# A token norm's factors one tile behind the evictions, low weights ahead of both, and sums a quarter into the second panel

## The reference, cut to what matters

```python
x = x + rms_norm(jnp.einsum("bse,ed->bsd", mix, w_out[layer]), attn_post_g[layer])
h2 = rms_norm(x, ffn_pre_g[layer])
f = conv_ffn(h2, w_up[layer], conv_w[layer], conv_b[layer], w_down[layer])
x = x + rms_norm(f, ffn_post_g[layer])
# the second block begins with rms_norm_2(x, g) and its input projection
```

## Time and profile before

| | us |
|---|---|
| median of 3 runs | 1391.78 (1391.68 to 1392.61) |
| the profiled execution | 1388.91 |
| its span, first to last instruction | 1386.8 |
| TensorE busy | 1317.0, 95% of the span |
| VectorE busy | 854.3, 62% |
| ScalarE busy | 579.3, 42% |
| GpSimd busy | 218.5, 16% |
| mean granted TensorE clock | 0.981 of full speed |

### The profile page before, as it was taken

How to read it: one execution, slowest core, us unless ns; L and a number is a source line. 1 busy time by engine, 2 the same in 40 slices (tenths; PEclk the granted TensorE clock), 3 DMA queues, 4 the chain that set the end, 5 groups by cost and what they waited for, 6 DMA issues and landing times.

```text
span 1386.8 us, 16092 instructions
## 1 busy us (share of the span) xinstructions
PE 1317.0 (95%) x5982; PEld 1031.8 (74%) x5982; DVE 854.3 (62%) x1497; ACT 579.3 (42%) x872; POOL 218.5 (16%) x173
## 2 busy tenths in 40 slices
PE   7999988899999999999999999899799989999996
PEld 6776656788888888888888868687678855658885
DVE  6355753788887388648853612569987256663342
ACT  5345645544333243224422534323564246653321
POOL 2322211000000000000000034220005411114450
PEclk9999999999999999999999999799899999999999
DMA  5211101122232222322223222311122210002411
GB/s 192 91 62 61 61 31 61 61 91 91 98 114 92 91 91 93 115 95 91 91 92 109 97 99 91 123 61 61 61 91 91 92 60 31 31 31 87 156 61 61
DMA packets 17788, 116.52 MB, mean 84 GB/s; under 512 B 1984, under 2 KB 2240, under 8 KB 4544
## 3 DMA queue, kind: packets, MB, share of 16 engines
q1 hardware_dynamic: 16320, 108.35, 22.0%
q10 hardware_dynamic: 1408, 7.37, 1.4%
HBM read 111.52 MB, written 4.19 MB: 83 GB/s over the span
## 4 chain that ended last, share of the span: by engine, by line
PE 80%; DVE 14%; ACT 3%; issue 2%; DMA 0%; DVEq 0%; ACTq 0%; SPq 0%
PE PG L352 16%; PE PG L354 16%; PE PG L353 16%; PE PX L494 4%; PE PX L763 3%; PE PX L429 2%; PE PX L428 2%; PE PX L430 2%; PE PG L429 2%; PE PG L428 2%; PE PG L430 2%; PE PG L792 2%; PE PX L671 1%; DVE WL L1296 1%; PE PX L802 1%
## 5 line engine op out<-in xcount | busy, mean ns | idle before, releaser
L352 PE MATMUL PG<-XH,WH 128*128 128x512 f32 x992 | 392.2, 395 | 14.5 <-DVE WL L1296 9.3
L332 POOL TENSOR_TENSOR WL<-RAW,WH 128x512 fp32r<-128x512 f32 x160 | 215.3, 1376 | 1135.7 <-ACT WH L850 1135.7
L353 PE MATMUL PG<-XL,WH 128*128 128x512 f32 x992 | 387.9, 391 | 0.0
L354 PE MATMUL PG<-XH,WL 128*128 128x512 f32 x992 | 387.7, 391 | 0.0
L850 ACT ACTIVATE WH<-RAW 128x2048 fp32r<-128x2048 f32 x100 | 191.4, 1914 | 374.8 <-PE PG L354 264.3
L352 PEld LDWEIGHTS PG<-XH,WH 128*128 128x128 f32 x992 | 187.4, 189 | 58.4 <-DVE WL L1296 11.9
L353 PEld LDWEIGHTS PG<-XL,WH 128*128 128x128 f32 x992 | 187.5, 189 | 39.9 <-issue 1.4
L354 PEld LDWEIGHTS PG<-XH,WL 128*128 128x128 f32 x992 | 187.3, 189 | 39.3
L1296 DVE TENSOR_TENSOR WL<-RAW,WH 128x2048 fp32r<-128x2048 f32 x60 | 137.2, 2287 | 52.1 <-ACT WH L850 51.9
L1052 ACT ACTIVATE Z<-Z 128x512 f32<-128x512 f32 x32 | 20.3, 633 | 164.7 <-DVE Z L1605 164.7
L1589 DVE TENSOR_TENSOR U<-PG,R 128x1024 f32<-128x1024 f32 x32 | 39.2, 1224 | 53.2 <-PE PG L354 48.5
(11 more groups left out here) (309 smaller groups left out, 2079.0 us busy)
## 6 DMA issues: line engine op xcount, KB each, us to landing
RAW<-panels SPq DMA_DIRECT2D x100, 1024.0 KB, 4.8
x_spill<-XT ACTq DMA_DIRECT2D x1, 2048.0 KB, 7.0
XT<-x_spill ACTq DMA_DIRECT2D x1, 2048.0 KB, 7.8
outT<-SQ SPq DMA_DIRECT2D x4, 512.0 KB, 3.0
XT<-xT ACTq DMA_DIRECT2D x2, 512.0 KB, 6.4
XT<-xT SPq DMA_DIRECT2D x2, 512.0 KB, 9.1
RGW<-rgw ACTq DMA_DIRECT2D x1, 1024.0 KB, 4.8
UK<-uk ACTq DMA_DIRECT2D x1, 512.0 KB, 5.8
```

The source lines that it names most:

```text
L332: ins = pool.tensor_tensor(WL[:, s].rearrange("p a b -> p (a b)")[:, piece], RAW[:, s, piece], WH[:, s].rearrange("p a b -> p (a b)")[:, p ...
L352: pe.matmul(o, WH[:, s, c, ms], xh[:, c, :], start=(c == 0), stop=False)
L353: pe.matmul(o, WH[:, s, c, ms], xl[:, c, :], start=False, stop=False)
L354: mm = pe.matmul(o, WL[:, s, c, ms], xh[:, c, :], start=False, stop=(c == DC - 1))
```

## The change

In both norms VectorE's stream is written in another order. The low weights of the next stage's first panel (`lo_ahead`) come first. Then tile 0 and tile 1 are evicted, and from there each tile's factor stands behind the eviction of the next tile; the factors of tiles 2 and 3 come last. Inside a factor the mean square goes to a scratch column of its own and stands ahead of the reciprocal, behind a wait for the tile's sum rather than for its root. TensorE's stream changes at one place in each of the two stages: the two products that sum the squares stand behind the first 12 matmuls of the second panel, not behind the first panel. The first stage of all, in1, keeps its order.

```diff
@@ one_panel @@
                     if chunk_done is not None and m == 1 and c < 2:
                         chunk_done(c)
+                    if quarter_done is not None and (m, c) == (0, 3):
+                        quarter_done()
                 mm.then_inc(panel_done, 1)
...
@@ gemm @@
-                peeled = 1 + max([-1, *after, 0 if ready else -1, 1 if p0 == 0 else -1])
+                peeled = 1 + max([-1, *after, *quarter, 0 if ready else -1, 1 if p0 == 0 else -1])
...
@@ gemm_norm @@
-                gemm(name, ready=(once(ready), 0),
-                     after={0: lambda: mean_square(norm, [(acc, 1, src[:, 0, :]), (acc, 1, src[:, 1, :])]), **more},
-                     chunk_done=chunk_done)
+                sums = {0: lambda: mean_square(norm, [(acc, 1, src[:, 0, :]), (acc, 1, src[:, 1, :])])}
+                if chunk_done is None:
+                    gemm(name, ready=(once(ready), 0), after={**sums, **more})
+                else:
+                    gemm(name, ready=(once(ready), 0), after=more, chunk_done=chunk_done, quarter={1: sums[0]})
...
@@ token_factor @@
-                v, r = MSV[:, t:t + 1], [RTK[:, 3 * t + k:3 * t + k + 1] for k in range(3)]
+                r = [RTK[:, 3 * t + k:3 * t + k + 1] for k in range(3)]
+                if t == 0:
+                    dve.wait_ge(once("tok_half"), TURN[norm] + 1)
+                dve.wait_ge(once("tok_sum"), 8 * TURN[norm] + NB + t + 1)
+                step_(dve.scalar_tensor_tensor(out=r[2], in0=SSB[:, t:t + 1], scalar=1.0 / 1024, in1=MSV[:, t:t + 1],
+                                               op0=ALU.mult, op1=ALU.add))
                 dve.wait_ge(once("tok_root"), 4 * TURN[norm] + t + 1)
                 link(dve.reciprocal(r[0], MSR[:, t:t + 1]))
-                link(dve.scalar_tensor_tensor(out=v, in0=SSB[:, t:t + 1], scalar=1.0 / 1024, in1=v,
-                                              op0=ALU.mult, op1=ALU.add))
-                link(dve.scalar_tensor_tensor(out=r[1], in0=r[0], scalar=v, in1=r[0], op0=ALU.mult, op1=ALU.mult))
+                link(dve.scalar_tensor_tensor(out=r[1], in0=r[0], scalar=r[2], in1=r[0], op0=ALU.mult, op1=ALU.mult))
...
@@ the tile loop of n2; that of n4 is changed alike @@
+            lo_ahead(p)
             for t in range(NB):
...
-                if t == 0:
+                if t == 1:
                     first_half("n2")
-                    lo_ahead(p)
-                token_factor("n2", t)
+                if t in (1, 2):
+                    token_factor("n2", t - 1)
+            token_factor("n2", 2)
+            token_factor("n2", 3)
```

More of the change, by code:

```diff
@@ L338, in _, with one_panel @@
         def _(pe):
-            def one_panel(p, s, xh=XH, xl=XL, ready=None, chunk_done=None):
+            def one_panel(p, s, xh=XH, xl=XL, ready=None, chunk_done=None, quarter_done=None):
                 pe.wait_ge(w_lo, p + 1)
@@ L371, in panel_piece, with gemm @@
                     mm.then_inc(panel_done, 1)
-            def gemm(name, xh=XH, xl=XL, ready=None, after={}, chunk_done=None):
+            def gemm(name, xh=XH, xl=XL, ready=None, after={}, chunk_done=None, quarter={}):
                 p0, _ = FIRST[name]
-                peeled = 1 + max([-1, *after, 0 if ready else -1, 1 if p0 == 0 else -1])
+                peeled = 1 + max([-1, *after, *quarter, 0 if ready else -1, 1 if p0 == 0 else -1])
                 for k in range(peeled):
-                    one_panel(p0 + k, (p0 + k) % 2, xh, xl, ready if k == 0 else None, chunk_done if k == 0 else None)
+                    one_panel(p0 + k, (p0 + k) % 2, xh, xl, ready if k == 0 else None, chunk_done if k == 0 else None,
+                              quarter.get(k))
                     if k in after:
@@ L1656, in down_last @@
                     lo((p0 + k) % 2, p0 + k + 3)
+                lo_ahead(p0 + 2)
                 for t in range(NB):
@@ L1663, in down_last @@
                     dve.tensor_tensor(dst, PG[:, (t + 2) % NB, :], dst, ALU.add).then_inc(once("tok_y") if t < 3 else evac, 1 + t // 3)
-                    if t == 0:
+                    if t == 1:
                         first_half("n4")
-                        lo_ahead(p0 + 2)
-                    token_factor("n4", t)
+                    if t in (1, 2):
+                        token_factor("n4", t - 1)
+                token_factor("n4", 2)
+                token_factor("n4", 3)
             down_out(0)
```

## The result

| | before | changed |
|---|---|---|
| median of the first five runs | 1391.68 (1388.72 to 1392.61) | 1381.52 (1377.90 to 1386.44) |
| ratio, 95% interval | | 0.9928 [0.9908, 0.9948] |
| profiled execution, its span | 1388.91, 1386.8 | 1386.44, 1384.3 |
| mean clock of the profiled execution | 0.981 | 0.978 |

I had forecast 1384.6 in a range of 1382.2 to 1388.2. The median lies 3.1 us under the forecast and 0.7 under the range. The profiled execution is not the median: it is the slowest of the five, at the lowest clock of them.

The account below looks back on a forecast made before the run. TensorE was taken as the bound, losing time in waits at the norms and sums. 2.98 + 0.48 + 1.80 + 1.80 + 0.2 = 7.26, taken as 7.2 off 1391.78: 1384.6 us, eight-in-ten range 1382.2 to 1388.2.

Parts of the forecast that it names:

- Numbers: Whole kernel: forecast at chance 0.62, own range 1383.2 to 1386.2, including about 0.5 us of spread between runs.
- rival 3: Clock falls at other places; a stretch of some 2.5 us goes or comes: 1382.1 or 1387.1, chance 0.11.
- The local sum: Gains in n2, n4 and at both places of the sums: 7.26 us, taken as 7.2.
- Low weights first: In n2, low weights run before tile 0's eviction, moving it from 230.70 to 232.46 at no cost; cover 0.5 us.
- n2, 2.98 us: In n2, group three starts 2.98 us earlier, with TensorE's own groups deciding and everything behind the first chunk moving equally.
- n4, 0.48: In n4, group three loses its 0.56 us wait, group two starts 0.08 later: gain 0.48 us.
- The sums, 1.8 and 0.1 each: In up0 and in2a, TensorE's wait for the sums goes, 1.8 us each, plus 0.1 each for products inside a stream.
- The cover of 0.92 us: Sums' input comes at 260.58, TensorE reaches them after 12 matmuls at 261.50, so nothing is waited.
- What could take it back: VectorE's later low weights, for panel 15 in up0: cover falls from 3.9 to 1.2 us; in in2a about 3 us.
- Rival 1: VectorE becomes the bound behind the sums, TensorE stops before panel 15: gives back 3.6 us, 1388.2, chance 0.13.
- Rivals 2, 4 and 5: Evictions don't lead, 1388.0, chance 0.07; new clock fall inside the change, 1397.6, 0.03; no effect, 1391.8, 0.04.

Follow-up runs that it names:

- base_again: The kernel before, unchanged, timed against itself: median 1392.51 us over 11 executions, ratio 1.0002.
- experiment 7: The change with the sums behind 6 matmuls of the second panel instead of 12: TensorE waits again, shown as 0.27 us in up0, 0.21 in in2a.
- warm_xr: The change plus 9 products on constants in front of xr alone: median 1382.79 us, ratio 0.9933.
- warm: The change plus products on constants: one behind each of 24 index units, 8 before xr, 28 before rg's first panel: 1409.62 us, ratio 1.0128.
- warm_rg: The change plus only the 28 products on constants in front of rg's first panel: 1386.02 us, ratio 0.9950.

## Why the prediction was wrong

*Where it failed.* The step is in "Numbers": "about 0.5 us of spread between runs", with rival 3, the clock falling at other places, at a chance of 0.11 and one stretch of 2.5 us. I had three runs within 0.9 us and took that for the spread. Single executions of the unchanged kernel spread over 6.4 us (60 of them, 1388.03 to 1394.39), those of the change over 9.1 (16, 1377.90 to 1386.97), and both go with the mean clock, by some 1.0 to 1.1 us for each 0.001. The local sum was nearly right, 7.26 against 7.54 us; what failed is the term for everything else. The profiled execution before, 1388.91 at 0.981, told it: 2.9 us under its own median, and I only carried it along. A median of five draws from such a spread misses by 1 to 2 us for no other reason. The first difference of medians was 10.2 us, the next two 7.5 and 7.9; by those two the forecast would have been within 0.7 us. So the first median was a lucky draw for the change; with that spread a hit within 1.5 us would have been in part luck too.

*What is shown of the cause.* The span of a trace divides into eight stretches, each from one matmul of TensorE to another. Their lengths in us, for two traces of the kernel before, the first of the change, and the ten traces without filler products:

| stretch | `before` | `base_again` | change | all ten |
|---|---|---|---|---|
| start to out1's last matmul | 238.43 | 239.85 | 241.90 | 236.96 to 242.75 |
| to the third panel of up0 (changed) | 37.86 | 37.81 | 32.76 | |
| to dn3's last matmul | 500.25 | 500.25 | 500.25 | 500.25 |
| to behind in2a's second panel (changed) | 35.34 | 35.33 | 32.89 | |
| to xr's first matmul | 85.22 | 85.18 | 85.22 | 85.17 to 85.22 |
| xr | 46.23 | 45.07 | 45.29 | 45.07 to 46.23 |
| rg and wr, to the attention's first product | 171.86 | 171.83 | 171.80 | 171.80 to 171.86 |
| to the last instruction | 271.59 | 273.93 | 274.18 | 271.59 to 274.29 |

Outside the two changed stretches only three move, and the kernel before differs from itself there by 1.4, 1.2 and 2.3 us. In these traces there is no third place that the change made faster. The shortest value that any of the ten has of each row, with the change's 32.76 and 32.83 in its two, adds up to a span of 1376.4 us and the longest to 1386.3; the change's 16 spans are 1375.8 to 1384.8. The two sums, over pieces of different executions, are estimates, but they cover the 16 within 0.6 us without another cause.

In the 14 traces that I have, of kernels alike up to n2, out1's last matmul comes anywhere from 236.96 to 242.75, though all issue the same until there; the windows show half-clock stretches at different places of the attention. The stretches of the change don't take part: from out1's last matmul to the first XT all nine traces with the change's order have 4.89 or 4.90 us, at whatever time out1 ended. In the xr stage the traces of before and with parts of the change have 45.1 to 46.2 us, again the same code.

*What stays open.* What sets off a fall of the clock in one execution and not in the next, and whether the change also shifts the odds of the falls. Its 16 executions have a mean clock of 0.9804 and the 60 of before 0.9788; at equal clock they differ by some 6.7 us, a little less than the 7.54 that the stretches gained. Mean clock isn't an exact measure, since a fall under another engine's work, as in rg, costs nothing. The three traces of the change itself are all of long executions, 1386.2 to 1386.6; I have none of its shortest.

*Low weights first.* Right: tile 0 cost nothing, and the evictions of tiles 1 to 3 followed TensorE at once. But their place is worth little, 0.3 us once the evictions lead; I had given the low weights as the start of the delay.

*n2, 2.98 us.* Measured 3.22. Two small things: the reciprocal follows the moved instruction after 0.06 us (242.94 and 243.00), not 0.20, and VectorE takes the first chunk 0.42 us behind group three's start now that TensorE runs through, not 0.53.

*n4, 0.48.* Measured 0.64. DG of tile 2 is there 2.16 us behind dn3's last matmul (before 2.12), so group two is 0.04 us later, not 0.08; group three starts 0.53 us earlier (4.55 against 5.08), and VectorE takes its chunk 0.11 us sooner behind it, as in n2. The bound was right: TensorE's own groups.

*The sums, 1.8 and 0.1 each.* Measured 1.90 and 1.88 alone. The cover of 0.92 us was measured by its removal (experiment 7).

*What could take it back.* Rival 1 did not come: WL of panel 15 was done at 273.41, 1.25 us ahead of TensorE's need at 274.66 (I had 1.2). VectorE evicted panels 14 to 16 late and waited for TensorE again at panel 17:

```profile
271.12 2.29 DVE L1301 TENSOR_TENSOR WL<-RAW,WH 128x2048 fp32r<-128x2048 f32 x1 [0.58 <-ACT WH L855]
...
307.50 1.22 DVE L1600 TENSOR_TENSOR U<-PG,R 128x1024 f32<-128x1024 f32 x1 [1.05 <-PE PG L354]
```

Rivals 2, 4 and 5 did not come either: the clock stayed at 1.00 in both stretches. Rival 3 is the one that came, but not for its reason. I had tied a new or missing fall to everything coming 7.2 us earlier; the largest differences, 236.96 to 242.75, lie ahead of the change, and its price of 2.5 us was for one stretch where three can move.

My reading of the Trainium skill (TensorE: Matmul & The Clock Gate, "The HAM clock gate"), that activity releases the throttle, fits the 9 products ahead of xr only in part: in `warm_xr` the clock was back before they began (0.82 granted in 884 to 888, the products from 886.81), and they kept it at 1.00. It did not hold for the filler among the index units, where a TensorE shown busy for 40 of 40 us stayed at 1.2 GHz. The page's remark that the place differs from run to run is what the runs bear out most, and I had given it too little room.

## What to carry to other kernels

Where one engine alternates between an eviction and a chain that waits for another engine's answer, put the next eviction ahead of the chain: the answer's time then passes under work. A reduction that only later work needs can stand some matmuls into the next panel; its cover is counted in matmuls, and taking half of these away measures it. And when a profiled execution and the median differ by 0.2% at different clocks, that difference is the spread that a forecast has to carry: compare stretches of the trace, not medians, for a gain of that size.

## What the runs showed that I had not expected

- In `warm`, TensorE was shown busy in all of a 40 us window, with 102 matmul records, at a granted clock of 0.50 throughout; index products (64 contracted rows) and products on constants (128x128) took turns. The panel behind the last 9 products on constants ran at 2.4 GHz from 921.43 on.
- A half clock that costs nothing: rg's third panel began at 1.2 GHz in the change (0.63 us a matmul) and at 2.4 in `warm_rg` (0.40), and the stage took 113.2 us both times.
- Two small VectorE instructions that don't depend on each other start 0.06 us apart (242.94, 243.00), with a link between them 0.19 to 0.26.
